# A two-block network on one core: the convolution's row groups gated one slot sooner, and the last attention head's weights all loaded ahead

## The reference

```
# layer 1: convolution
u = h @ w_in + b_in ;  a, ga, z = split(u, 3)
c = causal depthwise conv of (a * sigmoid(ga)), 31 taps, + b_dw
c = silu(layer_norm(c, norm_g, norm_b))      # over the 1024 channels of a token
y = (c * silu(z)) @ w_out + b_out

# layer 2: gated linear attention (GLA), 4 heads, chunks of tokens
q, k, v, r, a1 = split(h @ w_in)
g = log_sigmoid(a1 @ w_a2 + b_a) / 16        # decay per channel
o_t = q_t S_t ;  S_t = exp(g_t) * S_{t-1} + k_t^T v_t
y = (rmsnorm(o) * silu(r)) @ w_out

# layer 3: banded attention beside a multi-scale pool, gated, then w_out
```

## Time and profile before

| | |
|---|---|
| median of the runs | 2378.11 us |
| the profiled execution | 2377.62 us, span 2375.9 us, mean granted clock 0.985 |
| PE busy | 2291.1 us (96%) |
| DVE busy | 1474.2 us (62%) |
| ACT busy | 1127.2 us (47%) |
| POOL busy | 867.1 us (36%) |
| row slots of the convolution | about 540 to 760 us of the span |
| GLA, passage to head 2, to head 3 | about 1113 to 1140, 1280 to 1315 us |

### The profile page before, as it was taken

How to read it: one execution, slowest core, us unless ns; L and a number is a source line. 1 busy time by engine, 2 the same in 40 slices (tenths; PEclk the granted TensorE clock), 3 DMA queues, 4 the chain that set the end, 5 groups by cost and what they waited for, 6 DMA issues and landing times. The chain is left out here.

```text
span 2375.9 us, 35211 instructions
## 1 busy us (share of the span) xinstructions
PE 2291.1 (96%) x13534; PEld 1178.1 (50%) x13534; DVE 1474.2 (62%) x2412; ACT 1127.2 (47%) x2182; POOL 867.1 (36%) x661
## 2 busy tenths in 40 slices
PE   8999999998988999999999998999999999999998
PEld 4555555543444445555554554444655555444443
DVE  7999999976674245545445444677467777245422
ACT  7766666586763234435334333333256666333211
POOL 3988888878784111111101100344033333000000
PEclk9999999999999999999999998999999999999999
DMA  5011111033334400100100001323200000102222
GB/s 207 28 47 43 45 45 36 32 127 112 129 102 148 89 1 6 54 1 6 45 1 14 1 1 72 116 98 116 70 21 10 19 2 1 41 18 83 87 106 89
DMA packets 52221, 134.71 MB, mean 57 GB/s; under 512 B 5391, under 2 KB 23439, under 8 KB 51032
## 3 DMA queue, kind: packets, MB, share of 16 engines
q1 hardware_dynamic: 52056, 132.46, 16.8%
HBM read 96.65 MB, written 35.80 MB: 56 GB/s over the span
## 5 line engine op out<-in xcount | busy, mean ns | idle before, releaser
L1177 DVE SCALAR_TENSOR_TENSOR cv_tap_sum<-cv_glu,cv_prm,cv_tap_sum 128x1024 f32<-128x1024 f32 x326 | 418.8, 1288 | 11.9 <-ACT cv_tap_sum L672 2.4
L931 POOL TENSOR_TENSOR mixed<-mixed,cv_tap_products 128x1024 f32<-128x1024 f32 x153 | 363.2, 2374 | 78.8 <-ACT cv_tap_products L687 63.3
L100 PE MATMUL cv_proj<-H_hi,cv_w_ga 128*128 128x416 f16 (+1 forms) x640 | 216.8, 339 | 8.0 <-DVE H_lo L1150 8.0
L101 PE MATMUL cv_proj<-H_lo,cv_w_ga 128*128 128x416 f16 (+1 forms) x640 | 216.8, 339 | 0.0
L102 PE MATMUL cv_proj<-H_hi,cv_w_ga 128*128 128x416 f16 (+1 forms) x640 | 216.6, 338 | 0.0
L102 PE MATMUL gm_vr<-gm_wvr_hi,H_lo 128*128 128x512 f16 (+1 forms) x544 | 203.4, 374 | 0.0
L101 PE MATMUL gm_vr<-gm_wvr_lo,H_hi 128*128 128x512 f16 (+1 forms) x544 | 203.4, 374 | 0.0
L100 PE MATMUL gm_vr<-gm_wvr_hi,H_hi 128*128 128x512 f16 (+1 forms) x544 | 203.3, 374 | 0.0
L1848 POOL TENSOR_TENSOR gm_q_inter<-gm_q_rel,gm_block_decays 128x512 f32<-128x512 f32 x16 | 16.8, 1048 | 448.3 <-ACT gm_block_decays L1927 423.8
L687 ACT ACTIVATE cv_tap_products<-cv_glu,cv_prm 128x1024 f32<-128x1024 f32 x138 | 151.6, 1138 | 35.5 <-POOL mixed L931 35.4
L2435 POOL TENSOR_TENSOR at_probs<-at_probs,at_rsum 128x768 f32<-128x768 f32 (+1 forms) x64 | 90.4, 1412 | 163.8 <-DVE at_rsum L2719 163.8
(11 more groups left out here) (464 smaller groups left out, 5736.4 us busy)
## 6 DMA issues: line engine op xcount, KB each, us to landing
cv_w_stage<-conv_w SPq DMA_DIRECT2D x24, 512.0 KB, 4.1
mixed<-gla_w SPq DMA_DIRECT2D x8, 1024.0 KB, 9.1
go_rows<-h_rows SPq DMA_DIRECT2D x16, 512.0 KB, 4.0
h_rows<-go_rows SPq DMA_DIRECT2D x16, 512.0 KB, 2.8
pl_sums_a<-h_rows SPq DMA_DIRECT2D x16, 512.0 KB, 3.5
out<-pl_sums_a SPq DMA_DIRECT2D x16, 512.0 KB, 2.6
cv_tap_products<-gate_z SPq DMA_DIRECT2D x24, 256.0 KB, 3.1
mixed<-xT SPq DMA_DIRECT2D x12, 416.0 KB, 8.6
```

What stands on the lines that cost most here:

```text
L100: nc.tensor.matmul(out, w_hi, x_hi, start=first, stop=False)
L101: nc.tensor.matmul(out, w_hi, x_lo, start=False, stop=False)
L931: nc.gpsimd.tensor_tensor(c_unit(U), c_unit(U), prod[:, r % 3, :], ALU.add).then_inc(s_add, 1)
L1177: nc.vector.scalar_tensor_tensor(out=acc_unit(U), in0=window(U, k), scalar=col(U // 2, k), in1=acc_unit(U), op0=ALU.mult, op1=ALU.add).the ...
```

## The change

In the convolution, each of the groups 2 to 4 has its first two units (k = 0, 1) in the slot of the group's totals (slots 1, 4 and 8, `FIRST_UNITS`), and the other six in the slots behind: group 2 three in slot 2 and three in slot 3 (before: 3, 3 and 2 in slots 2 to 4), group 3 two each in slots 5 to 7 (before: 5 to 8), group 4 in 9 to 11 (before: 9 to 12). The first two units stand in each queue thus: DVE normalises them behind `finish` and ahead of the row's residual; ACT makes their silus ahead of the row's square root, their highs behind the row's normalise; POOL gates them and makes the lows at the end of its slot, behind the bias add; SP loads their gates at the end of its slot. DVE's normalising of the other six is in two lots of three. All low halves are made by POOL; DVE's are gone, with their semaphore.

In GLA, all four last pieces of head 3 are loaded when the wide ones are, each with its own semaphore: pieces 8 and 9 into the columns of the last token group in tiles 4 and 5 of M, which are head 2's, pieces 10 and 11 into `wst`. ACT waits, before it stores chunk 13 of head 2 (the first chunk of the last token group), for the low half of piece 9.

```diff
-        NORMS = {2: (2, range(4)), 3: (2, range(4, 8)), 5: (3, range(4)), 6: (3, range(4, 8)), 9: (4, range(4)),
-                 10: (4, range(4, 8))}
-        UNITS_AT = {0: (1, range(2, KT)), 2: (2, range(3)), 3: (2, range(3, 6)), 4: (2, range(6, 8))}
-        UNITS_AT.update({4 * T + u - 7: (T, range(2 * u, 2 * u + 2)) for T in (3, 4) for u in range(4)})
-        LOWS_AT = {3: (2, (5,)), 4: (2, (6, 7)), 7: (3, (4, 5)), 8: (3, (6, 7)), 11: (4, (4, 5)), 12: (4, (6, 7))}
-        DVE_LOWS = [T * KT + k for T, ks in LOWS_AT.values() for k in ks]
+        NORMS = {2: (2, range(2, 5)), 3: (2, range(5, KT)), 5: (3, range(2, 5)), 6: (3, range(5, KT)), 9: (4, range(2, 5)),
+                 10: (4, range(5, KT))}
+        UNITS_AT = {0: (1, range(2, KT)), 2: (2, range(2, 5)), 3: (2, range(5, KT))}
+        UNITS_AT.update({4 * T - 8 + u: (T, range(2 * u, 2 * u + 2)) for T in (3, 4) for u in range(1, 4)})
+        FIRST_UNITS = {s: (T, range(2)) for (s, h), T in TOTALS.items()}
...
@@ SP: the row loop, behind load_row(s + 1)
+                    T, ks = FIRST_UNITS.get(s, (0, ()))
+                    for k in ks:
+                        load_gate(T, k)
@@ ACT: the row loop
                     if (s, 1) in SUMS:
                         copy_sums(SUMS[s, 1])
+                    T, ks = FIRST_UNITS.get(s, (0, ()))
+                    for k in ks:
+                        silu(T, k)
                     if s < NS:
...
                             mm.then_inc(s_u, 1)
+                    T, ks = FIRST_UNITS.get(s, (0, ()))
+                    for k in ks:
+                        high(T, k)
@@ POOL: gated and the row loop
-                        if i and T * KT + ks[i - 1] not in DVE_LOWS:
+                        if i:
                             low(T, ks[i - 1])
-                    if len(ks) and T * KT + ks[-1] not in DVE_LOWS:
+                    if len(ks):
                         low(T, ks[-1])
...
                     if s + 1 < NS:
                         add_bias(s + 1)
+                    gated(*FIRST_UNITS.get(s, (0, ())))
@@ PE
-                        wait_low(pe, (T + 1) * KT)
+                        pe.wait_ge(c_lo, (T + 1) * KT)
@@ DVE: the row loop
-                    if s in LOWS_AT:
-                        T, ks = LOWS_AT[s]
-                        for k in ks:
-                            gated_low(T, k)
...
                             if (s, h) in TOTALS:
                                 finish(TOTALS[s, h])
+                                normed(*FIRST_UNITS[s])
@@ GLA
+            if a >= WIDE_PIECES and hd == GH - 1:
+                c0 = group_cols(SEQ // GROUP - 1)[0]
+                return M[:, (2 * hd - 2 + a - WIDE_PIECES) * L + c0:(2 * hd - 2 + a - WIDE_PIECES) * L + c0 + NPIECE]
...
-            return room(hd, q, q + 1) if hd < GH - 1 or q < WIDE_PIECES else wst[:, q % 2, :]
+            return room(hd, q, q + 1) if hd < GH - 1 or q < WIDE_PIECES + 2 else wst[:, q % 2, :]
...
-                        for q in (WIDE_PIECES, WIDE_PIECES + 1):
-                            sp.dma_start(wst[:, q % 2, :], w_heads[hd, :, q * NPIECE:(q + 1) * NPIECE]).then_inc(s_w[q % 2], 16)
+                        for q in range(WIDE_PIECES, PIECES):
+                            sp.dma_start(staged(hd, q), w_heads[hd, :, q * NPIECE:(q + 1) * NPIECE]).then_inc(s_wp[q - WIDE_PIECES], 16)
                     sp.wait_ge(s_lg, hd * NG)
                     sp.wait_ge(s_x, hd * NG)
                     sp.dma_start(wg[:, :], w_gate[hd]).then_inc(s_wg, 16)
-                    if hd == GH - 1:
-                        for q in (WIDE_PIECES + 2, WIDE_PIECES + 3):
-                            sp.wait_ge(s_wl, 2 + hd * PIECES + q - 1)
-                            sp.dma_start(wst[:, q % 2, :], w_heads[hd, :, q * NPIECE:(q + 1) * NPIECE]).then_inc(s_w[q % 2], 16)
...
-                                act.wait_ge(s_w[q % 2], 16 * ((q - WIDE_PIECES) // 2 + 1))
+                                act.wait_ge(s_wp[q - WIDE_PIECES], 16)
...
                     act.wait_ge(s_ot, ROW(hd, c))
+                    if hd == GH - 2 and c == 13:
+                        act.wait_ge(s_wl, 2 + (GH - 1) * PIECES + WIDE_PIECES + 2)
```

More of the change, by code:

```diff
@@ L303, in conv_layer @@
         c_d, c_n, c_sl, c_m = m.sem("c_centred"), m.sem("c_normed"), m.sem("c_silu"), m.sem("c_gated")
-        c_hi, c_lo, c_lod = m.sem("c_hi"), m.sem("c_lo"), m.sem("c_lo_by_dve")
+        c_hi, c_lo = m.sem("c_hi"), m.sem("c_lo")
         c_sz = [m.sem(f"siluz_loaded{k}") for k in range(KT)]
@@ L490, in units @@
                 eng(T, k)
[L492 to L497, removed]
         def wait_h(eng, s):
@@ L752, in silu @@
                         if k >= R0:
-                            wait_low(act, n - R0 + 1)
+                            act.wait_ge(c_lo, n - R0 + 1)
                     elif n >= KT + R:
-                        wait_low(act, n - R + 1)
+                        act.wait_ge(c_lo, n - R + 1)
                     else:
@@ L1275, in _ @@
                 taps(last + 11, last + 15)
-                def gated_low(T, k):
-                    dve.wait_ge(c_hi, T * KT + k + 1)
-                    nc.vector.tensor_tensor(c_half(T, k, 1), silu_at(T, k), c_half(T, k, 0), ALU.subtract).then_inc(c_lod, 1)
                 def last_taps():
@@ L1684, in gla_mix @@
         p_kd, p_ot, p_att = p_at[:, P:2 * P], p_s[:, DV:2 * DV], p_o[:, DV:DV + P]
-        s_w = [m.sem("w_loaded_even"), m.sem("w_loaded_odd")]
+        s_wp = [m.sem(f"last_w_loaded{q}") for q in range(4)]
         s_wh, s_wl, s_wg = m.sem("w_hi_done"), m.sem("w_lo_done"), m.sem("gate_w_loaded")
```

## The result

The changed kernel takes **2358.6 us** (median of 6 runs, 2357.65 to 2362.28); the kernel before took 2377.7 beside it (6 runs, 2376.32 to 2378.81). The ratio is 0.9923, 95% interval 0.9910 to 0.9935. A second set of runs, of the same kernel, gave 2358.96 (2357.84 to 2364.43), ratio 0.9917 (0.9904 to 0.9931). The forecast was 2364.0, in 2358.5 to 2371.5: the direction was right, and the time stands 0.1 above the lower bound.

The account below looks back on a forecast made before the run. PE, busy 96% of the span, was taken as the bound, so only its waits and lowered clock matter. 2377.6 - 6.7 (GLA) - 7.7 (convolution) = 2363.2, plus 0.5 for the median: 2363.7, said as 2364; range 2358.5 to 2371.5.

Parts of the forecast that it names:

- GLA's passage: Passage to the last head (head 3) falls from 23.54 to 16.88, as measured at head 2: 6.66 us gained.
- the grown wait for row 1: Convolution, group 2: POOL readies row 1 at 584.4 instead of 580.83; PE's wait grows from 4.6 to 8.2.
- the three waits that go: Convolution: PE's waits for last low halves before rows 5, 9 and 13, 11.9 us in all, vanish.
- rival D: Convolution: row 1's wait doesn't grow and the new waits don't come; 2358.6 us, chance 0.10.
- Rows 5, 9, 13, 16: Convolution: row 5 starts 0.4 later than before, later rows sooner, the sum 9.4 us earlier at row 16.
- The waits at the transposes of rows 4 and 8: Convolution, groups 3 and 4: new PE waits for POOL's scale and shift, 1.8 and about 2 us.
- the walk: Following the convolution's engine queues in order, group by group: 9.4 us gained at row 16 before the charge for unknowns.
- the 1.7 charged for all unknowns: Convolution: charge for low clock after new waits, a longer low stretch and small slot waits; 9.4 becomes 7.7.
- The sum takes nothing from it: Convolution: POOL freed from interference by DVE's 11 lows counted as no gain; trace showed 0.2 x 6 on POOL's side.
- B: Convolution's waits only move to the transposes of rows 1, 4 and 8, low clock with them; 2371.4 us, chance 0.12.
- C: The GLA wait stays because the chain of gate and masked scores is late anyhow; 2370.4 us, chance 0.04.
- E: Convolution: POOL bounds slots 1 to 12, its lows waiting for ACT's highs; slower by 5.2, 2383 us, chance 0.04.

Follow-up runs that it names:

- e1: The changed kernel with its GLA part taken back, so the convolution part alone: 2364.67 us, ratio 0.9950 to the kernel before.
- e4: The kernel before with only the 11 low halves given from DVE to POOL, slots unchanged: 2372.59 us, ratio 0.9978.
- e3: The changed kernel with the 11 low halves left on DVE, one slot sooner than before: 2362.74 us, ratio 0.9939.
- e2: The changed kernel with its convolution part taken back, so the GLA part alone: 2375.44 us, ratio 0.9983 to the kernel before.
- e6: The changed kernel with POOL's scale and shift put ahead of the units in every slot: 2368.28 us, ratio 0.9956.
- e5: The changed kernel with POOL's scale and shift of row 1 put ahead of the units in slot 2 alone: 2364.24 us, ratio 0.9935.
- e9: The changed kernel with the row's work ahead of the units' on ACT and POOL in slots 2 and 3: 2359.11 us, ratio 0.9915.

## Why the prediction was right, and where its sizes were off

The mechanism was right: GLA's passage, the grown wait for row 1 and the three waits that go are all in the trace as described. The sum was 5.4 too high, and that the measured 2358.6 still lies in the range, by 0.1, is partly luck: its low end takes in most of rival D, whose first condition did not come true. Of the 5.4, 3.1 are the convolution's, 1.2 stand outside both parts in the profiles (1.0 in the table, which counts the convolution from row 2), and 1.1 come from rounding and from the medians, which don't lie to the profiled executions as was assumed.

**GLA, 6.66: exact.** The passage to head 3 became 16.88, the number read off the passage to head 2, in all nine traces that have this part; in those without, 22.9 to 23.5. Reading the price from a place where the same program text already ran without the wait gave the wait and its low clock together.

**Transposes of row 1: right.** Forecast 584.4, measured 584.62; this segment grew by 3.56, forecast 3.6. The wait itself is 6.48 and not 8.2 because PE came there 1.9 later, 1.7 of it from a low-clock stretch after row 2's start, which the trace of before didn't have there; in e1, without that stretch, the same wait is 8.2. This was the largest cost of the change and it came in full; rival D, whose time of 2358.6 the result meets exactly, had it not growing, so D was not what happened. Only its other half, that the new waits don't come, was nearly so.

**Rows 5, 9, 13, 16: the term that was mis-sized.** Forecast 603.65, 656.0, 703.2 and 735.8; measured 604.52, 655.41, 701.59 and 734.42. From the transposes of row 1 to row 5 it took 0.65 more than forecast, within the 1.6 allowed for a longer low stretch. The waits at the transposes of rows 4 and 8 were 0.16 and 0.87, not 1.8 and 2. Two things made them smaller: PE came to the first 1.2 later than the walk had it, and POOL was ready sooner, by 0.5 at row 4 and by some 1.4 at row 8; part of that is its price, 4.00 for scale and shift of a cv_glu row against 4.72 (row 2 was through at 599.3, not 599.8). And of the 1.7 charged for all unknowns only the 0.65 came: no low clock from row 5 to row 16. So the transposes ahead of row 16 came 10.8 earlier (11.0 counted from row 2), where the walk said 9.4 and the sum 7.7: 1.64 + 1.13 + 1.7 for the waits and the charge, less 0.87 for row 5 and 0.5 for rows a little longer than computed.

**The lows: a misreading that cost little in the sum.** "The sum takes nothing from it" was wrong. I had read 0.2 x 6 for the interference from the scale being slower than the shift behind it, as if the shift were undisturbed. Both were disturbed: the undisturbed price is 2.0, and it stood in the trace of before, in the bias add of the same shape on the same tile at 1996 ns. But the walk already had the lows on POOL and DVE free of them, so what it left out is only POOL's faster scaling, 0.7 per cv_glu row, of which 0.5 is seen in the wait at row 4. That e4 shows the move of the lows alone to be worth 5.7 in the old schedule, and e3 about 4 in the new one (3.2 in its two segments), says what this part of the change is worth, and not what the forecast missed: in e4 3.9 of it are waits before rows 5, 9 and 13 (11.9 before, 8.0 there), which the walk had going. The rule of the Trainium skill, page SBUF — State Buffer (Who interferes with whom), pointed the right way: by it the lows' removal would free POOL, and the trace after has 4.3 us of POOL time freed. The "some 11 us" of the prediction has no row behind it; nearest to it comes what the lows lost on DVE's side, estimated above at 10.2.

**The rest, 1.0 in the profile.** I gave 1.6 to either side for low stretches falling otherwise. At the end of GLA alone the low time was 13.7, 17.1, 20.5, 23.9 and 27.3 us in different traces, with segments from 44.0 to 46.6; at two places behind it, 1670 to 1700 and 2020 to 2050 us, the traces of e1, e2, e3 and e6 have 3.4 more at the low clock each time and are 1.2 to 1.5 longer; e2's median stands 4.4 above its expectation with its mechanism intact. The allowance was too small by a factor of two or three. The medians differ by 19.1, the profiles by 18.7; whether the 0.4 between them is this too, the runs don't tell.

**Rivals.** B and C fell with the traces. E's ingredient was there: POOL idles 2.46 in the slots of first units, waiting for highs, at the place and with the length named (2.6). Its condition was not: the silus did come a slot sooner, and idle before gates fell by 22.

## What to carry to other kernels

To price the removal of a stall, look for the place where the same instructions already run without it; that number held to a hundredth in its segment, though e2's median shows less than half of it. To see whether an engine is being slowed by another, compare an operation with one of the same shape on the same tile at another time, not with its neighbour, which may be slowed as well; and look at both engines, as here the one that gave the work away had lost more than the other. When two queues hold up the same step, moving work in one of them only renames the wait: e5 changed POOL's order and nothing came of it, e9 changed both and the next consumer (the sums) was late.

## What was not expected of the hardware

- DVE subtractions with two SBUF inputs slow GpSimd's 128x1024 float32 operations of two tensors beside them from 2.00 to 2.45 us in the mean (cv_glu tiles), and from 2.36 to 2.58 in e3 (cv_w_stage). The cv_w tiles take 2.35 even undisturbed, the cv_glu tiles 2.00, in the same operation and shape; no run here says why. The subtractions themselves took 1605 ns in the mean on DVE, against 680 for one of the same size with an operand in PSUM.
- Waits of 0.2 to 0.9 at rows 4 and 8 brought no low clock. Around the wait of 6.48 for row 1, which ended at 584.62, the mean granted clock of 580 to 590 was 0.66.
- The low stretches at the end of GLA come to 13.7 (e1) to 27.3 us (e2) in kernels whose PE work there is the same, and the segments differ by 2.6.
